# Routing and experts as one block, slot lists from one-hot products, expert rows added in the next layer's load

## What is computed

```python
u = rmsnorm(x, norm1_g)
proj = u @ w_in
# four mixers of 4 heads of width 64, per-head QK RMS norm:
# A latent attention (dense causal), B dilated windows (3 branches merged),
# C forgetting attention (dense causal), D sliding window 128 with sinks
h = x + mix @ w_o
return h + hierarchical_moe(rmsnorm(h, norm2_g), w_rg, b_rg, w_re, b_re, w1, w3, w2)
```

## Time and profile before

| | |
|---|---|
| median of 3 runs | 2380.35 us (2380.16 to 2383.33) |
| profiled execution | 2379.22 us, its span 2377.4 us |
| mean granted TensorE clock | 0.949 |
| TensorE busy | 2150.3 us, 90% of the span |
| VectorE | 694.5 us, 29% |
| ScalarE | 557.5 us, 23% |
| GpSimd | 310.5 us, 13% |
| DMA | 355.69 MB, mean 150 GB/s |

### The profile page before, as it was taken

How to read it: one execution, slowest core, us unless ns; L and a number is a source line. 1 busy time by engine, 2 the same in 40 slices (tenths; PEclk the granted TensorE clock), 3 DMA queues, 4 the chain that set the end, 5 groups by cost and what they waited for, 6 DMA issues and landing times. The chain is left out here.

```text
span 2377.4 us, 28217 instructions
## 1 busy us (share of the span) xinstructions
PE 2150.3 (90%) x9724; PEld 1199.3 (50%) x9724; DVE 694.5 (29%) x1697; ACT 557.5 (23%) x1309; POOL 310.5 (13%) x356
## 2 busy tenths in 40 slices
PE   7999969999996899999389999799999959999992
PEld 4555536666454444444155555456564534444441
DVE  0111145545243122222311110455452332222223
ACT  1211135545211011111021211455461110111110
POOL 0221120100011000000211221201000110000002
PEclk9999979999997899999789999799999969999996
DMA  6000000020423999999710000000101229999996
GB/s 222 18 18 0 0 27 19 1 76 6 130 79 115 348 368 369 365 367 368 266 37 18 18 0 0 27 19 5 73 6 56 72 71 341 369 364 365 374 350 256
DMA packets 212771, 355.69 MB, mean 150 GB/s; under 512 B 19136, under 2 KB 162368, under 8 KB 212672
## 3 DMA queue, kind: packets, MB, share of 16 engines
q1 hardware_dynamic: 183232, 269.93, 32.4%
q0 software_dynamic: 14848, 50.36, 6.3%
q10 hardware_dynamic: 14592, 34.11, 3.6%
HBM read 303.88 MB, written 50.48 MB: 149 GB/s over the span
## 5 line engine op out<-in xcount | busy, mean ns | idle before, releaser
L399 PE MATMUL banks<-r_win,r_tile 128*128 128x384 f32 (+3 forms) x1536 | 530.0, 504 | 9.7 <-DMA r_win<-in_w_in 7.6
L1590 PE MATMUL banks<-r_proj 128*128 128x512 f32 x1024 | 454.9, 597 | 4.6 <-DVE r_proj L1645 4.6
L399 PEld LDWEIGHTS banks<-r_win,r_tile 128*128 128x128 f32 x1536 | 292.0, 192 | 226.5 <-issue 63.9
L1590 PEld LDWEIGHTS banks<-r_proj 128*128 128x128 f32 x1024 | 191.3, 192 | 222.8 <-issue 216.9
L1197 PE MATMUL banks<-r_proj 128*128 128x512 f32 x512 | 231.2, 607 | 5.2 <-DVE r_proj L1285 5.2
L1577 PE MATMUL banks<-r_proj 128*128 128x512 f32 x512 | 230.5, 593 | 3.0 <-ACT r_proj L1630 3.0
L935 ACT ACTIVATE r_win<-r_win 128x256 f32<-128x256 f32 (+7 forms) x256 | 177.3, 696 | 16.6 <-DVE r_win L1006 13.9
L859 PE MATMUL banks<-fixed,r_win 128*128 128x128 f32 x984 | 168.5, 290 | 0.0
L876 PE MATMUL banks<-r_win,r_proj 128*64 128x128 f32 x1968 | 168.0, 287 | 0.2
L844 PE MATMUL banks<-r_win 64*128 64x512 f32 (+3 forms) x704 | 146.4, 509 | 16.8 <-DVE r_win L981 13.5
L1197 PEld LDWEIGHTS banks<-r_proj 128*128 128x128 f32 x512 | 97.5, 195 | 119.4 <-issue 119.4
(11 more groups left out here) (165 smaller groups left out, 1760.0 us busy)
## 6 DMA issues: line engine op xcount, KB each, us to landing
r_proj<-in_w SPq DMA_DIRECT2D x192, 1024.0 KB, 10.1
expert_rows<-r_proj ACTq DMA_DIRECT2D x64, 512.0 KB, 7.0
r_win<-in_w_in SPq DMA_DIRECT2D x6, 1536.0 KB, 19.9
r_proj<-in_w_o SPq DMA_DIRECT2D x2, 4096.0 KB, 13.6
normed<-r_proj SPq DMA_DIRECT2D x16, 512.0 KB, 3.4
out<-r_tile SPq DMA_DIRECT2D x16, 512.0 KB
r_tile<-in_x SPq DMA_DIRECT2D x8, 512.0 KB, 3.8
r_win<-in_w_in SPq DMA_DIRECT2D x2, 2048.0 KB
```

Source lines behind the costliest of these rows:

```text
L399: mm = pe.matmul(bk[b][:, 0:CHUNKS[c]], uT[j][:, k, :], w_ch[c][:, k, :], start=(k == 0), stop=(k == KT - 1))
L1590: mm = pe.matmul(bk[2 + j][:, 0:2 * F], xT[j][:, k, :], w13[j][:, k, :], start=(k == 0), stop=(k == KT - 1))
```

## The change

`out_route` and `experts` become one function and one block, `route_experts`.

- Routing. h itself, and not its normalised form, is transposed and stored (to a DRAM tensor `residual`, once a tile); 1/rms is multiplied into the router's logits, into silu's scale and into the product of the hidden halves. The slot lists are no longer scattered into a table in DRAM: VectorE writes one-hot matrices (`place1`: the slot of each token, 128 columns; `code`: token number and target row for the chosen expert, 64 columns), and TensorE sums their products over all tiles in a PSUM bank (`sum_slots`). The same with gates and 1/rms (`gate_r`, `sum_gates`). What no token fills is given the number SKIP = 4096, beyond the bounds of the indirect DMAs, which then skip this row. The zeroed table and the token numbers loaded for it are gone. The order of TensorE in a tile is written out by hand, in eighths of the next tile's output projection (`more`).
- Experts. GpSimd gathers from `residual` and now also stores the expert rows, by an indirect DMA to the place of their token (`scatter`); it goes gather(e), scatter(e-2), gather(e+1). The rows are multiplied by their gates when they are evacuated (`first_half`, `second_half`). At the end of each pair of experts VectorE writes the one-hot matrices for the next pass (`next_slots`, five instructions) and TensorE adds their product into a bank, whether or not a next pass comes. The loop over passes is now inside each engine's part of the block.
- Between the layers. `project` of the second layer loads, for each tile, h and two expert rows a token (four loads for these, into the places in `r_proj` that the tile's own projection will fill later), VectorE adds them in two passes of 768 and 256 columns each (`add_rows`, called at the start of `evac_x`), and TensorE's transposes, ScalarE's squares and the store to `out` wait for the sums. After the last layer plain loads take the place of the gathers L1551, and the two additions a tile and the stores follow as before.
- Attention. Query blocks 0 to 3 of a head pair are taken two in a step, in the sliding-window pairs all of them: 44 steps instead of 64. All transposes of a step come first and then all values of the step before.

```diff
+def load_y(sp, s, g, t):
+    for n, (a, b, place) in enumerate(y_places(s, t)):
+        sp.dma_start(place, s.y_dram[(n // 2 * s.NT + t) * P:(n // 2 * s.NT + t + 1) * P, a:b]).then_inc(
+            g.x[t % 2].sem, 16)
...
+            eng.wait_ge(g.xa.sem, g.xa.at(layer - 1, 4 * (2 * i + j + 1)))
...
+                if layer > 0:
+                    sp.wait_ge(g.xa.sem, g.xa.at(layer - 1, 4 * (t + 1)))
+                    sp.dma_start(s.out_f[t * P:(t + 1) * P], x_t[j]).then_inc(g.xs[j].sem, 16)
...
+            def add_rows(i, j):
+                t = 2 * i + j
+                dve.wait_ge(g.x[j].sem, x_loads(s, layer, i))
+                for n, (a, b, place) in enumerate(y_places(s, t)):
+                    if n >= 2:
+                        dve.wait_ge(g.xa.sem, g.xa.at(layer - 1, 4 * t + n - 1))
+                    nc.vector.tensor_tensor(x_t[j][:, a:b], x_t[j][:, a:b], place, ALU.add).then_inc(g.xa.sem, 1)
...
+                if layer > 0:
+                    add_rows(i, j)
...
+            blocks = [[qb, qb + 1] for qb in range(0, nt // 2, 2)] + [[qb] for qb in range(nt // 2, nt)]
...
-                parts = len(st.groups)
-                for n in range(parts):
+                for n in range(len(st.groups)):
                     transpose_weights(st, n)
-                    if st.i > 0:
-                        values(steps[st.i - 1], n, parts)
-                for pair, half in norm_at(st.pair, st.qb, NT):
+                if st.i > 0:
+                    values(steps[st.i - 1])
...
+def route_experts(nc, s, g, layer):
...
+                    out=xg[e % 2], out_offset=None, in_=s.h_dram,
+                    in_offset=bass.IndirectOffsetOnAxis(ap=slot_rows[:, e:e + 1], axis=0),
+                    bounds_check=NT * P - 1, oob_is_err=False).then_inc(g.gx[e % 2].sem, 16)
...
+            def scatter(e):
+                nc.gpsimd.indirect_dma_start(
+                    out=s.y_dram, out_offset=bass.IndirectOffsetOnAxis(ap=slot_rows[:, E + e:E + e + 1], axis=0),
+                    in_=y_t[e % 2], in_offset=None,
+                    bounds_check=2 * NT * P - 1, oob_is_err=False).then_inc(g.ys[e % 2].sem, 16)
...
+                for e in range(E + 2):
+                    if 2 <= e < E:
+                        wait_alone(pool, s, g.xt.sem, g.xt.at(done, e - 1))
+                    if e < E:
+                        gather(e)
+                    if e >= 2:
+                        wait_alone(pool, s, g.ya.sem, g.ya.at(done, e - 1))
+                        wait_alone(pool, s, g.yv.sem, g.yv.at(done, e - 1))
+                        scatter(e - 2)
...
+            def sum_slots(t):
+                pe.wait_ge(g.pl.sem, g.pl.at(layer, PLACE_STEPS * (t + 1)))
+                for k in range(2):
+                    mm = pe.matmul(bk[7][:, 0:2 * E], place1[t % 2][:, k, :],
+                                   code[t % 2][:, k].rearrange("p c e -> p (c e)"),
+                                   start=False, stop=(t == NT - 1 and k == 1))
+                mm.then_inc(g.tb.sem, 1)
...
+                more(0)
+                transpose_h(t)
+                more(1, 2)
+                if t > 0:
+                    sum_slots(t - 1)
+                router_logits(t)
+                more(3, 4)
+                if t > 0:
+                    sum_gates(t - 1)
+                more(5)
+                count_pairs(t)
+                more(6, 7)
...
+                    pe.wait_ge(g.nv.sem, g.nv.at(done, i + 1))
+                    pe.matmul(bk[5][:, 0:4 * E], next_place, next_code, start=first(i),
+                              stop=isinstance(i, int) and i == NP - 1).then_inc(g.nt.sem, 1)
...
+                    step(v.tensor_scalar(code[j][:, k, 0, :], masks[j][:, k, :], s.tokens[:, 2 * t + k:2 * t + k + 1],
+                                         None, ALU.mult))
...
+                link(v.tensor_reduce(rel[:, t, :], prod[j], AX.X, ALU.add))
+                step(v.tensor_scalar(place1[j][:, 0, :], s.iota, rel[:, t, 0:1], None, ALU.is_equal))
...
+            v.tensor_scalar(slot_rows, bk[7][:, 0:2 * E], SKIP, None, ALU.add).then_inc(g.ix.sem, 1)
...
+                    v.tensor_scalar(y_t[j][:, 512:1024], bk[7][:, :], slot_gates[:, bass.ds(e, 1)], None,
+                                    ALU.mult).then_inc(g.yv.sem, 1)
...
+                def next_slots(i):
+                    here = bass.ds(i, 1)
+                    if not first(i):
+                        dve.wait_ge(g.nt.sem, g.nt.at(done, i))
+                    v.tensor_scalar(next_place, s.iota, flat[0][:, here], None, ALU.is_equal)
+                    for c, val in enumerate((s.tokens, s.targets, flat[2], flat[3])):
+                        ins = v.tensor_scalar(next_code[:, E * c:E * (c + 1)], s.iota[:, 0:E], flat[1][:, here],
+                                              val[:, here], ALU.is_equal, ALU.mult)
+                    ins.then_inc(g.nv.sem, 1)
...
+                            evac_tokens(i + j, 1 - j)
+                        if not (first(i) and j == 0):
+                            second_half(i - (1 - j), 1 - j)
+                    next_slots(i)
```

More of the change, by code:

```diff
@@ L854, in transpose_weights @@
                 at, count = st.groups[n]
-                heads = 1 if at + count <= st.nb else 2
-                pe.wait_ge(g.ex.sem, g.ex.at(layer, 2 * st.i + heads))
+                ready = sum(it.at < at + count for it in st.items)
+                pe.wait_ge(g.ex.sem, g.ex.at(layer, items_to(st.i - 1) + ready))
                 bank = take("w", (st.i, n))
@@ L1489, in experts, with pair_of, take @@
-    cidx, geff, vc = small[:, 2].bitcast(I32), small[:, 3], small[:, 4]
-    NP = E // 2
-    table_r = s.table.rearrange("(r p e) o -> r p (e o)", p=P, e=E)
+    NP = E // 2
+    last_layer = layer == s.L - 1
+    def pair_of(at, n):
+        return [w[:, at + j * n:at + (j + 1) * n] for j in range(2)]
+    x_t = pair_of(8192, D)
+    hT = [a.rearrange("p (k n) -> p k n", k=KT) for a in pair_of(10240, D)]
+    squares = w[:, 21248:21248 + D]
+    at = [12288]
+    def take(n, dt=F32):
+        at[0] += n
+        assert at[0] <= 14848
+        return w[:, at[0] - n:at[0]].bitcast(dt)
@@ new lines, in sum_gates @@
+            def sum_gates(t):
+                pe.wait_ge(g.gv.sem, g.gv.at(layer, GATE_STEPS * (t + 1)))
+                last = t == NT - 1
+                to = bk[3][:, 0:2 * E] if last else bk[7][:, 2 * E:4 * E]
+                for k in range(2):
+                    mm = pe.matmul(to, place1[t % 2][:, k, :], gate_r[t % 2][:, k].rearrange("p c e -> p (c e)"),
+                                   start=(last and k == 0), stop=(last and k == 1))
+                mm.then_inc(g.tg.sem, 1)
+            pe.matmul(bk[7][:, 0:4 * E], s.ident[:, :], bcast(s.junk[:, 0:1], [P, 4 * E]), start=True, stop=False)
@@ new lines, in _ @@
+            dve.wait_ge(s.project_sems.late.sem, s.project_sems.late.at(layer, 48))
+            v.memset(gl[:, :, NG:8], NEG)
+            v.memset(upto_now[1], 0.0)
+            for t in range(NT):
+                h_tile(t)
+                evac_hT(t)
+                choose(t)
+                place(t)
+                if t + 1 < NT:
+                    weigh(t)
+            dve.wait_ge(g.tb.sem, g.tb.at(layer, NT))
+            v.tensor_scalar(slot_rows, bk[7][:, 0:2 * E], SKIP, None, ALU.add).then_inc(g.ix.sem, 1)
@@ L1698, in tables @@
+def tables(seq):
     import numpy as np
```

1190 lines of the change are left out of this document (583 added, 607 removed).

## The result

The changed kernel takes 2573.17 us (median of 4 runs, 2571.03 to 2579.39), the kernel before beside it 2380.26 us: 1.0818 times, 95% interval 1.0803 to 1.0833. It is 193 us slower where 32 were forecast, and lies above the range (2470). The profiled execution has a span of 2569.2 us, 191.8 more than before.

What follows compares the result with a forecast made beforehand. TensorE, busy in nearly all of each long stretch, was taken as the bound. Terms 61 - 10 - 22 - 29 + 30 + 5 - 1.5 = +33.5 us gave span 2411, time 2412.5 us; range 2366 to 2470.

Steps and rivals of the forecast that it cites:

- Experts, gathers: Expert loop: gathers queued behind scatters on GpSimd land in 3.7 to 4.7 us, no TensorE stall; between 0 and 80 us.
- The rival on this: Expert loop: gathers land too late, deciding from 4.7 us on; 1.5 us a pair, 31 pairs, 2459 us; chance 0.15.
- The rival of a skip that does nothing: Expert gathers and stores: skipped rows still pass as descriptors, load and landing unchanged, 2.6 us a pair, 2493 us; chance 0.05.
- Experts, the wait for the slots: End of each expert pair: TensorE waits for VectorE's `next_slots`, 2.0 us a pair, +61 us in all.
- Second projection: Second layer's projection: six tiles wait 5.1 us for VectorE's additions, +30 us, and clock lost behind them, +5 us.
- Routing and its gap: Output projection with routing +8 us a layer, gap behind it 24 instead of 42.4; -22 us in all.
- Between the layers: From the last expert's rows to the second layer's first matmul: 16.8 instead of 46.5 us, -29 us.
- the end: After the last expert rows: plain loads replace gathers but the same bytes move, -1.5 us, between -6 and +4.
- Attention: Attention: fewer changes between transposes and values save 34.7 us a layer, PSUM bank waits cost 29.7; net -10 us.
- The gather's upper bound of 80 us: Expert loop: upper end of the 0 to 80 us allowed for TensorE stalls on gathers.
- the wait's of 85: End of each expert pair: +85 us if computing register offsets costs as much as one instruction each, 2.8 us a pair.
- Slower: Whole kernel: the changed kernel takes longer than before, by more than the 0.2% a measurement can tell; chance 0.77.

Runs made afterwards that it cites:

- the second experiment: On the changed kernel, VectorE's `next_slots` moved from the end of a pair to behind the evacuation of the first expert's transposes; 2465.53 us, 1.0368 times the kernel before.

## Why the prediction was wrong

**Experts, gathers (predicted 0, measured 46 us a layer alone).** This is the step that failed: "I take 3.7 to 4.7 and no stall". Both sides of it were off. The room was 3.8 us and not 4.7: in the pair above the gather goes out at 2125.22 and TensorE is free at 2129.05, since GpSimd issues the scatter only 0.9 us after the evacuation has ended (2123.02) and the gather 1.3 us behind it. And the landing took 6.0 us and not 3.7 to 4.7. The reasoning was that half the rows make a transfer shorter and that freer DMA engines bring it near the 4.3 of the earlier trace rows.

The run with full gathers shows that the number of rows does not matter, and the run with the gather first that its order with the scatter doesn't. The 4.2 us of the gather that runs alone show what the forecast took for granted: that the gathers of the loop would be like that one. What sets it apart, the scatter beside them or the busier engines, is open. The lighter load may have counted for something: with DMA at 0.71 the middle value is 6.0, with 0.99 it was 8.2; but it is 5.2 with 0.79 and 6.3 with 0.87, so the load alone does not set it. In the changed kernel the step cost 37.0 us a layer (472.3 less 435.3).

The rival on this had the mechanism and the point from which it decides, 4.7 us. It even named the wait, 2.3 us in one expert of each pair; measured were 2.36, without the first of each layer (70.8 / 30). But it went into its time with 1.5 us a pair, without a reason, and with no clock. The rival of a skip that does nothing was half right: the skipped rows do pass through the queue, but the bytes are saved (DMA 0.99 to 0.71), and the landing fell from 8.2 to 6.0, not to what the bytes would give. The Trainium skill ("DMA: Bandwidth & Descriptors", Anatomy of one DMA — SWDGE path) gives 2.0 us + bytes / 436 GB/s, by estimate 3.2 us for the full gather; 5.7 was measured, and for half of it 6.0, so that here neither the constant nor the slope fits.

**Experts, the wait for the slots (predicted 2.0 us a pair, measured 3.9).** The wait came as described, at its place, with 1.93 us (61.8 / 32), and with some 0.3 for the new matmul it is near the 2.0 of the sum. This is the second step that failed: the clock behind the wait was put at nothing. With this wait alone TensorE's busy time is 29 us a layer longer (399.5 against 370.4), some 24 to 26 of it by the clock (0.94 against 1.00 over 435.3 us). The prediction priced the clock behind the additions and not behind the same kind of wait here. Some 0.2 a pair more is "issue", 3.7 us a layer. It shows only in the runs in which TensorE waits just before the end of the loop's body, and is gone in those with `next_slots` in the idle stretch; that it is the jump back, no longer hidden by queued work, is a guess.

**Second projection (predicted +30 and +5, measured +44).** The additions cost 4.8 to 4.9 us, six times; 5.1 was worked out. The clock took 14, where 0 to 24 had been allowed and 5 taken. The rule of the Trainium skill that was put beside it ("TensorE: Matmul & The Clock Gate", Part 1), by which every such stall pays, with some 15 us more in the sum, was nearer; the granted clock of 0.95 against 0.99 agrees with it for these stalls of 4.8 us. In the experts it does not tell the cases apart: behind waits of 1.9 us the 16 instructions of L1503 ran slow 27 times in 30 in the run with the early gather and 4 times in 30 in the run with the gather first, and behind the 58 waits of 1.27 us of the second experiment the expert rows ran slow twice.

**Routing and its gap (predicted -22, measured -24.7).** The stage took 137.2 us, 139.5 were forecast. The gap is 24.0 us, as worked out, but by two errors that cancel. These rows of the changed kernel are the last count, the first gather and its transposes:

```profile
751.47 0.64 PE L1419 MATMUL banks<-r_proj,fixed 128*128 128x32 f32 x2 [2.19 <-DVE r_proj L1628]
...
756.10 1.20 POOL L1358 DMA_INDIRECT r_proj<-residual,rs  x1 [10.49 <-DVE rs L1700]
...
763.08 1.97 PE L1479 MATMUL banks<-fixed,r_proj 128*128 128x128 f32 x8 [5.73 <-DMA r_proj<-residual,rs]
```

The rows of the gather were there 7.0 us after its issue, not 3.7, the same mistake as in the loop (here it is a second gather that goes out 1.5 us behind it); the choice of the last tile was done 4 us sooner than counted (9 us from the last residual to the count, where the parts gave 13).

**Between the layers (predicted -29, measured -26.5), the end (-1.5, -2.6).** Right in mechanism and size.

**Attention (predicted -10 in all, measured -3).** Both terms are there, and both were too large by about the same share. TensorE's busy time in layer 1 went from the 275.1 us of this row of the kernel before to 250.4, 25 us instead of the 34.7 for fewer changes (some 2 us of it are the clock, 0.98 to 0.99), and the waits for the ring banks are 20.4 us a layer instead of 29.7. Only half of these, 10.2, are the waits for VectorE's copy that the prediction described; the other half are 30 short waits a layer for ScalarE's, which it did not have.

```profile
320.40:607.40 287.00, 275.10 (x2388) 174.39 (x2388) 151.09 (x393) 148.26 (x368) 27.61 (x21) 0.98 0.06 21
```

The 0.17 of idle in the earlier trace rows stands in rows of the weight loads, not of TensorE's matmul instructions, so the gain came as busy time. That the net stayed near zero is luck: two errors of one size in opposite terms.

**The chances.** Slower had 0.77 and came true; the range ended at 2470. The gather's upper bound of 80 us and the wait's of 85 were never added, though both hang on holes in the same stream of TensorE. Even with them the end would have been 2412.5 + 80 + 24, some 2517 us. What is then missing is mostly the clock in the experts, some 37 us in two layers, and the breaks that come with it, some 22; no bound had either.

## What to carry to other kernels

A gather on GpSimd needs a slot of time from issue to landing that is taken from a row under the same kind of load and with the same neighbours in its queue, here some 6 us; skipping half of its rows did not shorten it. Where one engine's instruction stream holds a store and the next load, ask what the load waits for through the store, and let the store lag by one more step: that was worth 74 us here, and moving five small VectorE instructions into an idle stretch 108 us. And a hole in a stream of matmuls that is otherwise full can cost more than its length: here the waits and the idle beside them were 71.0 us a layer (35.5, 30.9 and 4.6), and TensorE's busy time grew by 29.8 on top.

## What the runs showed of the hardware

- Indirect DMAs whose rows lie out of bounds still pass through the queue as packets, of 4 bytes each: 18432 packets with and without skipping, 33.60 or 50.36 MB, landing 6.0 and 5.7 us.
- The gathers' time from issue to landing had a middle value of 5.2 to 6.3 us in all runs of the changed kernel and its variants, with the scatter issued just ahead or just behind, with half or all of the rows. The one that ran alone, with the DMA engines 0.22 to 0.27 busy, took 4.2.
- TensorE's clock in the experts of layer 2, with the same instructions: 1.00 without waits, 0.99 with a wait of 1.27 us in nearly every expert, 0.94 with one of 1.93 us in each pair, 0.96 with both that and 2.36 us for a gather, and 0.99 with 1.88 us and 1.23 us for a gather. So the length of the waits does not order the runs, and the same wait can cost clock nearly every time or seldom; what sets this was not tried.
